# One queue or two for the selected pages: all requests of the sample attention move to SyncE

## The reference, cut to what matters

```python
def nsa_core(q, q_pos, kc_blk, vc_blk, gather_sel, n_sel_blocks, kvw, kw_pos):
    ...
    _, idx = lax.top_k(score, min(N_SEL, n_sel_blocks))
    kv_g = gather_sel(idx)
    ...
    s_s = jnp.einsum('bqgrd,bgqnkd->bgrqnk', q, kv_g[..., 0, :]) * scale
    ...
    o_s = jnp.einsum('bgrqnk,bgqnkd->bqgrd', p_s.astype(dt), kv_g[..., 1, :])
    s_w = jnp.einsum('bqgrd,bkgd->bgrqk', q, kvw[:, :, 0]) * scale
```

## Time and profile before

| what | us |
|---|---|
| median of three runs | 1059.35 |
| profiled execution, its own time | 1064.42 |
| its span, first to last instruction | 1062.8 |
| PE busy in the span | 961.1 |
| VectorE busy | 604.5 |
| GpSimd busy | 69.5 |

### The profile page before, as it was taken

The page is one execution under the profiler, slowest core; times in us unless marked ns, Lnnn a source line. Parts: engine busy times, 40 slices in busy tenths (PEclk is TensorE's granted clock), DMA queues, the critical chain, the costliest instruction groups (busy, mean ns, idle before and its releaser), DMA issues. The chain is left out here.

```text
span 1062.8 us, 17643 instructions
## 1 busy us (share of the span) xinstructions
PE 961.1 (90%) x6514; PEld 597.2 (56%) x6514; DVE 604.5 (57%) x1423; ACT 314.5 (30%) x785; POOL 69.5 (7%) x120
## 2 busy tenths in 40 slices
PE   5999999999968999999999996777999878888897
PEld 3576676777644445567556443454565556565443
DVE  3205897779255566999200004458787468878213
ACT  4310000110151033112111113446777445555002
POOL 0000000000000000000000006120000212211000
PEclk9999999999979999999999998888999989999999
DMA  8533653564153343576210111165200779885202
GB/s 341 202 75 120 195 157 86 158 198 142 33 184 101 94 123 119 148 181 193 80 68 18 73 40 60 52 245 221 71 1 2 246 260 314 290 285 199 100 0 89
DMA packets 48560, 147.80 MB, mean 139 GB/s; under 512 B 9433, under 2 KB 23130, under 8 KB 41818
## 3 DMA queue, kind: packets, MB, share of 16 engines
q1 hardware_dynamic: 43354, 129.89, 38.2%
q0 software_dynamic: 5120, 16.78, 4.7%
HBM read 139.63 MB, written 15.27 MB: 146 GB/s over the span
## 5 line engine op out<-in xcount | busy, mean ns | idle before, releaser
L1177 PE MATMUL PS<-arena 128*32 128x64 f32 (+15 forms) x5420 | 813.9, 379 | 31.6 <-issue 4.5
L1177 PEld LDWEIGHTS PS<-arena 128*128 128x128 f32 (+5 forms) x5420 | 470.0, 148 | 363.8 <-issue 219.1
L1180 PE MATMUL PS<-arena 128*128 128x128 f32 (+3 forms) x1094 | 158.2, 294 | 62.5 <-DVE arena L1937 14.4
L1180 PEld LDWEIGHTS PS<-arena 128*128 128x128 f32 (+3 forms) x1094 | 128.0, 150 | 93.7 <-issue 33.8
L2046 DVE SCALAR_TENSOR_TENSOR arena<-arena 128x576 f32<-128x576 f32 x8 | 6.5, 844 | 132.2 <-ACT arena L983 132.0
L1847 DVE TENSOR_TENSOR arena<-arena 128x2048 f32<-128x2048 f32 x32 | 73.2, 2289 | 2.0 <-DMA arena<-in_ccmp 0.8
L1848 DVE TENSOR_TENSOR arena<-arena 128x2048 f32<-128x2048 f32 x32 | 73.1, 2286 | 0.0
L1063 ACT ACTIVATE arena<-arena 128x512 f32<-128x512 f32 (+3 forms) x96 | 52.9, 554 | 22.7 <-DVE arena L2113 22.6
L2113 DVE CUSTOM_DVE_ANT_0 arena<-PS,arena 128x512 f32<-128x512 f32 (+3 forms) x96 | 41.4, 487 | 21.0 <-PE PS L1177 21.0
L504 POOL DMA_DIRECT2D arena<-in_csel x64 | 34.5, 539 | 220.8 <-PE PS L1180 110.1
L2006 DVE TENSOR_TENSOR arena<-arena,PS 128x512 f32<-128x512 f32 x16 | 11.0, 686 | 56.2 <-PE PS L1177 56.2
(11 more groups left out here) (193 smaller groups left out, 552.3 us busy)
## 6 DMA issues: line engine op xcount, KB each, us to landing
arena<-in_wall SPq DMA_DIRECT2D x19, 2048.0 KB, 8.6
arena<-in_ccmp SPq DMA_DIRECT2D x128, 256.0 KB, 3.7
arena<-in_csel POOLq DMA_DIRECT2D x64, 256.0 KB, 5.9
arena<-in_csel SPq DMA_DIRECT2D x64, 256.0 KB, 5.7
arena<-in_cmem SPq DMA_DIRECT2D x32, 256.0 KB, 3.8
arena<-in_win SPq DMA_DIRECT2D x8, 1024.0 KB, 10.3
out_win_s<-in_win SPq DMA_DIRECT2D x1, 8064.0 KB
arena<-in_xp SPq DMA_DIRECT2D x1, 2048.0 KB, 17.0
```

The costliest lines, as they stand in the source:

```text
L1177: return nc.tensor.matmul(out, lhsT, rhs, start=start, stop=stop, skip_group_check=True)
L1180: return nc.tensor.transpose(out, in_, ident[0:in_.shape[0], 0:in_.shape[0]])
```

## The change

SP issues all four pages of each quad, in the order that it had, with the same waits; the program of GpSimd ends after its last wait, with no page request. One semaphore per place counts all four pages, and PE waits for that alone.

```diff
-        sa_lo = [[sem(f"sa_pages01_{c}_{n}") for n in range(2 if c else 3)] for c in range(4)]
-        sa_hi = [[sem(f"sa_pages23_{c}_{n}") for n in range(2 if c else 3)] for c in range(4)]
+        sa_in = [[sem(f"sa_pages_{c}_{n}") for n in range(2 if c else 3)] for c in range(4)]
...
-            quad_load(sp, 0, 0, range(2), sa_lo)
-            quad_load(sp, 0, 1, range(2), sa_lo)
+            quad_load(sp, 0, 0, range(TILE), sa_in)
+            quad_load(sp, 0, 1, range(TILE), sa_in)
...
             for t in range(1, NB):
                 for c in range(1, 4):
-                    quad_load(sp, t, c, range(2), sa_lo)
+                    quad_load(sp, t, c, range(TILE), sa_in)
...
-            quad_load(pool, 0, 0, range(2, 4), sa_hi)
-            quad_load(pool, 0, 1, range(2, 4), sa_hi)
...
-            for t in range(1, NB):
-                for c in range(1, 4):
-                    quad_load(pool, t, c, range(2, 4), sa_hi)
...
-                            pe.wait_ge(sa_lo[k // 2][t % places], 32 * (t // places + 1))
-                            pe.wait_ge(sa_hi[k // 2][t % places], 32 * (t // places + 1))
+                            pe.wait_ge(sa_in[k // 2][t % places], 64 * (t // places + 1))
```

More of the change, by code:

```diff
@@ L658, in window @@
                              ).then_inc(sa_w[t % 3], 16)
-            quad_load(sp, 0, 0, range(2), sa_lo)
-            quad_load(sp, 0, 1, range(2), sa_lo)
+            quad_load(sp, 0, 0, range(TILE), sa_in)
+            quad_load(sp, 0, 1, range(TILE), sa_in)
             sp.wait_ge(pa_t, BANKS_OF_P * (UNITS - 2))
-            quad_load(sp, 0, 2, range(2), sa_lo)
+            quad_load(sp, 0, 2, range(TILE), sa_in)
             sp.wait_ge(pa_t, BANKS_OF_P * (UNITS - 1))
-            quad_load(sp, 0, 3, range(2), sa_lo)
+            quad_load(sp, 0, 3, range(TILE), sa_in)
             sp.wait_ge(pa_s, PT * UNITS)
@@ L668, in _ @@
             sp.wait_ge(pa_mix, 6)
-            quad_load(sp, 1, 0, range(2), sa_lo)
+            quad_load(sp, 1, 0, range(TILE), sa_in)
             window(1)
@@ L676, in _ @@
                         sp.wait_ge(state_out, 16)
-                    quad_load(sp, t + 1, 0, range(2), sa_lo)
+                    quad_load(sp, t + 1, 0, range(TILE), sa_in)
                     window(t + 1)
```

## The result

The changed kernel takes 1071.01 us, the median of 13 runs; the kernel before, 13 runs beside it, 1062.73 us. The ratio is 1.0074, interval [1.0052, 1.0096]: slower by some 7.9 us, less than 1%. Forecast were +2.0 us, and 1061.4 us from the three runs known then.

What follows compares the result with a forecast made beforehand. SP's issue of 16 pages and a window was to bound the sample attention at 18.76 us per trip (17.8 before); 4.0 us gained at the start, longer trips and a later last quad made +2.0 us, 1061.4 us, range 1054 to 1070.

Steps and rivals of the forecast that it cites:

- The interval: SP's time from one page request to the next, look-up and address work included: 1.146 us, extremes 1.097 and 1.204 us.
- The second rival: SP issues faster alone, below 1.080 us per page, and doesn't set the pace: -3.9 us, 1055.4 us; chance 0.17.
- the rule that was weighed: Skill rule that several issuing engines save only sequencer time, usually small beside the DMA; by it SP's issue sets no pace.
- the first stop: PE's 5.80 us wait for quad 1 before 855.88 us, at the sample attention's start; forecast to go, gaining 4.0 us.
- R2: Time SP's first page of trip 2 goes out (R: a trip's first page); forecast 862.34 us, before 866.31.
- The third rival: The stop at the start stays because the window alone holds up quad 1: +6.0 us, 1065.4 us; chance 0.13.
- What was put at nothing: Small parts counted as zero: GpSimd's 64 lost issues, one PE wait less per quad, window 0 delayed to 840.6 us.
- The loop with these: Sample attention trip: 8.02 us of issue, 2.9 landing, 0.1, then 6.75 give 17.8 us, under SP's own 18.76.
- K: Start of PE's 16 turns from key turn 4, which wait for quad 2; next trip's first page forecast 6.75 us later.
- the first rival: Landing stays 5.9 us, loop 20.8 us: +17 us, 1076 us; decides from a 3.9 us landing on; chance 0.10.
- R7: Time SP's first page of the last of these trips goes out; forecast 956.1 us, against 955.31 before.
- dear page interval: SP's page requests at the upper extreme of 1.204 us each through the sample attention: +7.8 us.

Runs made afterwards that it cites:

- the changed kernel's second trace: The changed kernel run again unchanged for another trace, against the kernel before: ratio 1.0074, stage 157.2 us, mean period 18.85 us.
- numbers ahead: The changed kernel, but SP reads eight page numbers (quads 1 and 2) ahead of the trip's wait: ratio to the kernel before 1.0051.
- Fixed pages: The changed kernel with page numbers fixed when the program is built, so no page-table look-up: ratio to the kernel before 0.9959.
- the second trace of the kernel before: The kernel before, run again unchanged for another trace of its sample attention: ratio 1.0001, stage 151.9 us, mean period 17.79 us.
- three windows: The changed kernel without the 1 MB loads of windows 3 to 7, an earlier loaded window being used: ratio to the kernel before 1.0041.

## Why the prediction was right and wrong

**Right: what becomes the bound.** Where PE doesn't hold it up, SP's issue sets the pace. The interval was 1.13 us (1.146 forecast). The mean period was 18.85 us in the changed kernel's second trace, with 2.7 us of waits for PE in the whole stage, and 18.87 us with numbers ahead, with none (18.76 forecast), and the kernel is slower, by less than 1%. Fixed pages show the cause from the other side. The second rival, that SP doesn't set the pace, falls with it, and so does the rule that was weighed: that the sequencer's time is "usually small relative to the DMA itself" (the Trainium skill, DMA: Bandwidth & Descriptors, section Issuing engines are not separate DMA queues) doesn't hold here, with 1.13 us of issue for 0.68 us of data; with fixed pages it was still 0.6 us.

**Right in part: the start.** The forecast had the first stop go, since nothing would compete with quad 1. It shrank, from 5.80 and 4.58 us in the two traces of the kernel before to 3.66 us in two parts (2.51 and 1.15) and 2.81 (2.54 and 0.27). What failed is the landing of 2.9 us for quad 1: its last page, requested 4.5 us after the 1 MB window in the same queue, took 5.8 us (844.49 to 850.26) and in the second trace 5.1. R2 comes 25.88 and 23.98 us after the start (23.77 forecast), before 27.74 and 25.81. So the gain is some 1.8 us between the means of two traces each, where 4.0 were forecast. The third rival, by which R2 stays at 27.74 us, falls. What was put at nothing stays there: GpSimd has no page left, and window 0, at 830.87 and 833.83 us, stops PE in neither trace.

**Wrong: the loop as a fixed 17.8 us.** This is the step *The loop with these*: landing 2.9 us, then 6.75 us from K to the next R, 1.0 us under SP's pace. Both terms were taken as constants at the value of an undisturbed trip.

- The landing that PE waits for is 3.11 to 4.18 us in eleven trips of the two traces of the changed kernel; for the last trip's quad 1 it is 4.95 us in one, and in the other the trip before has 7.35 us. The forecast had its own limit, 3.9 us, and charged it to the first rival alone, which supposed 5.9 us in every trip. In the first trace three of six trips lie beyond it, and those are the three where SP waits for PE. The landing alone is not enough for that: in the second trace one of 4.18 us, with turns at full clock behind it, ends in a trip of 18.88 us.
- From K to R took 9.17 us (853.10 to 862.27) and 9.19 us (894.02 to 903.21), not 6.75. Some 1.7 us of the 2.4 are the 16 turns at half the clock, 3.65 us for 1.94; the matmuls behind them have the rest. Work behind a stop can be slower than work without one, and no term of the sum had that. It is the larger part of the delay of both R2 and R4: SP, ready 1.19 us after the window's request, could have begun these trips at 859.58 and 900.03 and began them 2.69 and 3.18 us later; with 6.75 us from K it would have been 0.27 and 0.74 us. For the trip of 881.70 the sum with measured terms is 8.02 + 4.16 + 0.14 + 9.19 = 21.51 us; with the landing alone it would be 19.07, with the slow work alone 20.25.

So the loop goes from 17.8 to 22.1 us (the trip of 940.61, with the landing of 7.35), around a pace of 18.8, and the period is the longer of the two in each trip. The forecast of R2 to R7, 93.8 us, became 94.24 in the second trace and 100.46 in the first.

**Wrong: the last trip.** K was to follow R7 after 11.0 us; it took 13.13 in the first trace, with a stop of 2.64 us before 967.22 whose releaser no view names. In both traces the end of the stage comes some 39.0 us after R7, forecast 35.76 + 1.2 = 37.0. In the second some 1.3 us of the excess are late matmuls of sample 7 that run longer than in the first trace of the kernel before (2.25 us for 1.38, 1.56 for 1.09), at a granted clock of 0.59 from 987 to 991 us; the second trace of the kernel before has such too (2.24) and ends 37.17 us after R7, so they aren't the change's alone.

**The time itself.** 1071.01 us lies 9.6 us above the forecast, 1 us above the range. 3.4 us of these are the kernel before, whose median was 1059.35 us over three runs and 1062.73 over thirteen; the rest is the loop and the last trip. The change of +7.9 us lies in the range of -3 to +9 us that stood beside the forecast, where it was put down to a dear page interval: the size held and the reason didn't. The first rival's mechanism was at work, in some trips and not in all.

**Open.** The traces gave the stage +12.9 and +4.7 us over the kernel before's first, the median +7.9 us for the whole; how often each course is taken wasn't counted. Of the 8.2 us between the two traces, 5.6 us are longer busy time of PE for the same work (130.8 and 125.2 us in the stage; 125.2 before). Why one of sixteen equal pages lands late behind a window in one trip and not in the next no run tells apart. From K to the next R a trip with slow turns loses some 2.4 us in the changed kernel and 1.4 with three windows (8.3 us, against 6.9 with fast turns), but no run takes the half clock out and leaves the rest as it was.

## What to carry to other kernels

Multiply the requests of a period by what one costs its queue, look-up included (1.13 us here, of which fixed numbers save 0.5 us), and set that against the period: a queue with 57.7 us of waits has room, one with none becomes the pace. Where two paces lie within 1 us of each other, neither is the bound: put the spread of every term into both, and take the longer one trip by trip. Before giving up a second queue for the sake of one stop, look for what stands in front of the late transfer: moving one window behind one quad gained 0.4% and cost nothing.

## What was not expected of the hardware

- A later landing went with a shorter time: fixed pages land in a median of 5.1 us, those of the change in 3.4 us, and the first kernel is 1.1% faster. What counts is when the last page is there, not how long it was under way.
- A stop of TensorE can cost more than its length: the 16 turns behind stops of 2.51 and 1.15 us took 3.65 us at a granted clock of 0.50. In the second trace, behind stops of 2.46 and 1.11 us, they took 1.94 us, so the length of the last stops doesn't decide it alone.
- The same 8 windows requested by GpSimd made the kernel slower by another 0.8%, though that took eight requests from the queue that was the pace.
